# Joining the u and v tables of a PEER expert layer into one table of 8 KB rows, in a two-layer decoder step on one core

## The chip, the core and the metric

The kernel runs on one core of a Trainium2 chip. The metric is the device time of one execution in microseconds. Everything is float32. TensorE (PE in the rows) does matmuls into PSUM, VectorE (DVE) and ScalarE (ACT) the elementwise work, GpSimd (POOL) issues the gathers from HBM, SyncE (SP) issues the plain loads and stores. The core's 16 DMA engines carry all transfers.

## What is computed

Two layers over 256 prompt tokens and 8 sample tokens, width 1024. Each layer has a dense mixer (an mLSTM and a pooling group), a PEER expert layer, and a gated embedding. The expert layer is where the change sits. Each token picks 16 experts in each of 8 heads, so 128 of 16,384, and each expert has one row of 1024 floats in `u_tab` and one in `v_tab`:

```python
q = (xb @ wq).reshape(PEER_BLOCK, PEER_HEADS, 2, PEER_HALF)
s = jnp.einsum('thcd,chkd->thck', q, keys)
sv, si = lax.top_k(s, PEER_TOPK)
...
top, sel = lax.top_k(cand, PEER_TOPK)
eidx = jnp.take_along_axis(cidx, sel, axis=-1)
gate = jax.nn.softmax(top, axis=-1)
ue = u_tab[eidx]
act = jax.nn.gelu(jnp.einsum('td,thkd->thk', xb, ue))
ve = v_tab[eidx]
out = jnp.einsum('thk,thkd->td', gate * act, ve)
```

Over both layers that is 528 tokens x 128 experts x 2 rows of 4 KB, 553.7 MB out of 685 MB that the kernel moves.

## The kernel before, in words

The work is six tiles: 0 = A (tokens 0 to 127), 1 = B (tokens 128 to 255) and 2 = S (the 8 sample tokens) of layer 0, and 3, 4, 5 the same of layer 1. They run in four passes, `PASS_TILES = [[0], [1, 2], [3], [4, 5]]`. In a pass the dense front (`stage_front`: turn, norm, project, the mixer, mix, query, match, and the ranking steps rank, lists, pairs, best, soften, choose) leads to the indices of the experts. Then the experts are gathered and used, and the dense back (`stage_back`: turn3, gate, embed, apply, final) closes the layer.

Gathers. Each is one indirect DMA of 128 rows of 4 KB, one row to a partition, into a ring of `RING = 14` slots (`rows`, L1450). For a tile of 128 tokens, 128 gathers from `u` come first (gather i holds expert i of every token, so a token is a partition), then 128 from `v` (gather i holds all 128 experts of one token, so an expert is a partition). The order of all 1056 gathers is the list `GATHERS`. Gathers of u wait for the indices of their head (`best` and DVE's L2052), gathers of v for `turn_index`. Each waits also until its slot is free.

Use of a u slot. DVE multiplies it with the normed token, which ACT has put in two PSUM banks (`show`, L1633), and sums along the row (`take_dots`, L2105). The slot is then free. When all 128 products of a token are there, one gelu (L1642) and one product with the probabilities give the weights of the whole tile, PE transposes them, and DVE puts them in `wz`. Use of a v slot. PE multiplies four slots at a time (`GROUP = 4`, L1235) with 32-column windows of `wz`, two matmuls to a slot; the four slots are freed together. The sums pile up in `acc`, the same two banks that held the shown token. `add` then adds them to x, and only after it can the next tile be shown. In the last pass the last 24 tokens of tile 4 are handled in the lanes of the sample tile (`LATE`), so that the back of tile 4 can start earlier.

Order of the work. `make_schedule` weaves the list of gather steps (`groups_of`) with the dense steps, by a small table of costs (`STEPS`, `SMALL`, `ROW`, `FLIGHT`) that belongs to the kernel. Each engine then runs its part of the woven list in order. So while PE holds a dense step, the expert step behind it waits, and the other way round.

Weights. SP loads each half of a weight matrix (1 MB, 8 KB to a partition) in a ring of `WRING = 3` slots. One half, the first of the input projection, has a place of its own (`kept`) and is loaded once per layer.

## Time and profile before

| | us |
|---|---|
| three runs, median | 1912.31 |
| three runs, lowest and highest | 1903.66 and 1913.88 |
| profiled execution, first to last instruction (its span) | 1891.7 |
| DVE, POOL, PE busy in the span | 978.1, 998.2, 1079.0 |

The profile gives a span for its execution and no other time. The median of the runs stands 20.6 us above it, which covers what lies around the span and the difference between executions. The prediction sums in the span and adds those 20.6 us at the end. The rows in a later section show where the span goes. A row of a window gives start:end, length, then for PE, PE's weight loads, DVE, ACT and POOL the busy time with the number of instructions, then the granted TensorE clock (1.00 is 2.4 GHz, 0.50 is 1.2 GHz), the DMA's busy share, and GB/s. A row of a timeline gives start, length, engine and line, and in brackets the idle time before it. The trace counts each float32 matmul as two. In them, "idle before, releaser" is the time for which the engine stood still ahead of a group of instructions and who ended that; "share" of a DMA queue is the time that its packets took, as a share of 16 engines' time, and can pass 100% a little since packets overlap.

### The profile page before, as it was taken

How to read it: one execution, taken by the hardware profiler on the slowest of the kernel's cores; microseconds unless marked ns; L12 is line 12 of the kernel's file. 1: busy time of each engine (PE TensorE's matmuls, PEld its weight loads, DVE VectorE, ACT ScalarE, POOL GpSimd, SP SyncE). 2: the span in 40 equal slices, each digit the busy share in tenths (PEclk: the TensorE clock that was granted, in tenths of full speed). 3: DMA queues.
4: the chain of work that ended last, by engine and by line, in shares of the span. 5: the costliest groups of instructions: out<-in, count | busy, mean ns of one | idle time of the engine just before them, and what ended most of it. 6: DMA issues, size and time to landing. Idle time of an engine off the chain costs nothing. (4 is left out here: it accounts for less than half of the span.)

```text
span 1891.7 us, 17959 instructions
## 1 busy us (share of the span) xinstructions
PE 1079.0 (57%) x6318; PEld 499.7 (26%) x6318; DVE 978.1 (52%) x2585; ACT 192.3 (10%) x332; POOL 998.2 (53%) x1062
## 2 busy tenths in 40 slices
PE   8840257788955835385655874048885522045556
PEld 4420133433412422241112432024341211031113
DVE  1498975523445788954004576951344497850001
ACT  3200021201101200000000212000110000000002
POOL 0156534345465555656666353755446566656663
PEclk9965668789987967697676886578896765576678
DMA  8699869889999999989999799979999999999995
GB/s 333 244 359 379 337 244 410 337 359 399 357 360 406 423 410 421 404 343 419 371 366 386 256 421 365 408 286 418 368 337 366 402 374 381 396 330 372 368 367 206
DMA packets 172759, 685.11 MB, mean 362 GB/s; under 512 B 19616, under 2 KB 21344, under 8 KB 158190
## 3 DMA queue, kind: packets, MB, share of 16 engines
q0 software_dynamic: 152064, 553.72, 75.9%
q1 hardware_dynamic: 20606, 130.25, 17.3%
q8 instruction: 51, 0.84, 0.2%
q14 instruction: 38, 0.31, 0.0%
HBM read 677.66 MB, written 6.59 MB: 362 GB/s over the span
## 5 line engine op out<-in xcount | busy, mean ns | idle before, releaser
L2105 DVE SCALAR_TENSOR_TENSOR rows<-rows,acc 128x1024 f32<-128x1024 f32 x512 | 594.2, 1217 | 49.6 <-issue 26.7
L908 PE MATMUL bank<-wring,turned 128*128 128x512 f32 (+1 forms) x808 | 394.0, 635 | 40.6 <-DMA wring<-in_w 24.3
L1235 PE MATMUL acc<-rows,wz 128*32 128x512 f32 x1952 | 323.1, 783 | 143.6 <-DMA rows<-in_v,index_tb 102.6
L1450 POOL DMA_INDIRECT rows<-in_u,index_A x256 | 240.3, 939 | 303.2 <-DVE rows L2105 123.8
L1450 POOL DMA_INDIRECT rows<-in_v,index_ta x256 | 242.5, 947 | 234.1 <-PE acc L1235 142.2
L1450 POOL DMA_INDIRECT rows<-in_u,index_B x256 | 240.7, 940 | 179.1 <-DVE rows L2105 110.7
L1450 POOL DMA_INDIRECT rows<-in_v,index_tb x256 | 241.1, 942 | 138.7 <-issue 68.1
L908 PEld LDWEIGHTS bank<-wring,turned 128*128 128x128 f32 x808 | 160.5, 207 | 236.7 <-issue 205.7
L1235 PEld LDWEIGHTS acc<-rows,wz 128*32 128x32 f32 x1952 | 69.6, 130 | 351.9 <-issue 347.0
L1185 PE MATMUL bank<-xn_s,consts 128*128 128x128 f32 x256 | 48.6, 334 | 154.3 <-issue 154.3
L1185 PEld LDWEIGHTS bank<-xn_s,consts 128*128 128x128 f32 x256 | 42.9, 243 | 159.9 <-issue 159.9
L2151 DVE TENSOR_TENSOR x_b<-x_b,acc 128x1024 f32<-128x1024 f32 x2 | 2.4, 1222 | 155.8 <-issue 89.9
L905 PE MATMUL bank<-wring,turned_s 128*32 128x128 f32 x1568 | 64.9, 281 | 27.1 <-issue 27.0
L1959 DVE MAX8 top<-scratch 128x8 f32<-128x128 f32 x66 | 15.0, 282 | 120.9 <-ACT scratch L1604 119.6
L905 PEld LDWEIGHTS bank<-wring,turned_s 128*32 128x32 f32 x1568 | 44.8, 111 | 69.7 <-issue 69.6
L2141 DVE COPY wz<-w_later 128x64 f32<-128x64 f32 x4 | 0.9, 225 | 101.4 <-PE acc L1235 77.7
L1109 PE MATMUL bank<-consts,qk 128*128 128x128 f32 x64 | 12.5, 324 | 68.7 <-issue 66.3
L1194 PE MATMUL bank<-consts,dots_A 128*128 128x128 f32 x2 | 1.0, 476 | 76.6 <-issue 74.6
L2105 DVE DVE_READ_ACCUMULATOR rows<-rows,acc 128x1 f32 x512 | 42.0, 82 | 3.6 <-issue 3.6
L1136 PE MATMUL bank<-consts,top 128*128 128x128 f32 (+2 forms) x10 | 3.9, 393 | 61.9 <-DVE top_f L1993 61.9
L1259 PE MATMUL bank<-wring,emb 128*128 128x512 f32 x32 | 19.9, 781 | 26.8 <-issue 13.6
L2169 DVE TENSOR_TENSOR xn<-xn,bank 128x512 f32<-128x512 f32 x6 | 4.1, 689 | 59.9 <-PE bank L1259 59.9
(320 smaller groups left out, 1054.4 us busy)
## 6 DMA issues: line engine op xcount, KB each, us to landing
wring<-in_w SPq DMA_DIRECT2D x103, 1024.0 KB
out_sample<-scratch SPq DMA_DIRECT2D x2, 2128.5 KB
scratch<-in_c_s SPq DMA_DIRECT2D x2, 2064.0 KB
rows<-in_u,index_A POOLq DMA_INDIRECT x256
rows<-in_v,index_ta POOLq DMA_INDIRECT x256
rows<-in_u,index_B POOLq DMA_INDIRECT x256
rows<-in_v,index_tb POOLq DMA_INDIRECT x256
kept<-in_w SPq DMA_DIRECT2D x2, 1024.0 KB
```

The lines of the kernel that those rows point to most:

```text
L905: ins = pe.matmul(ps[lane_group(g), 0:P], turned["S"][:, 4 * h + c, :], w[:, c, g * P:(g + 1) * P], start=first, stop=end, skip_group_chec ...
L908: ins = pe.matmul(ps[:, part], turned["A"][:, 4 * h + c, :], w[:, c, part], start=first, stop=end, skip_group_check=True)
L1109: ins = pe.transpose(ps[:, i * P:(i + 1) * P], pq[:, 0, i * P:(i + 1) * P], const("ident"))
L1136: ins = pe.transpose(ps[0:m, i * P:(i + 1) * P], src[:, 2 * h0:2 * h1, :].rearrange("p l k -> p (l k)"), const("ident"))
L1185: ins = pe.matmul(ps[:, g * P:(g + 1) * P], const("ident")[:, lane:lane + 1].to_broadcast([P, P]), xn["S"][:, i * P:(i + 1) * P], start=Tr ...
L1235: ins = pe.matmul(acc[i * QUAD:(i + 1) * QUAD, c, :], wz[:, i, at:at + QUAD], row, start=first, stop=end, skip_group_check=True)
L1259: ins = pe.matmul(ps[:, :], emb[:, c, 0:P], w[:, 2 * j + c, :], start=(c == 0), stop=(c == 1))
L1450: pool.indirect_dma_start(out=rows[:, n % RING, :], out_offset=None, in_=a[table], in_offset=bass.IndirectOffsetOnAxis(ap=which[:, at:at + ...
L1959: highest = [marked(dve.max(values[:, 0:half], src)) for values, _, src in lists]
L2105: dve.scalar_tensor_tensor(u, u, 1.0, acc[:, :, :], ALU.mult, ALU.mult, accum_out=dots[kind][:, s:s + 1]).then_inc(u_used, 1)
L2151: after(dve.tensor_tensor(sum_, sum_, acc[:, :, :], ALU.add), acc_read)
L2169: free(dve.tensor_tensor(sig, sig, ps[:, 0:n], ALU.mult), "embed", t, j)
```

## The change

One table `uv` has the row of u and the row of v of an expert side by side, 8 KB. A gather brings 128 such rows into one of `RING = 8` slots of 8 KB a partition. There are 528 gathers in place of 1056. The ring takes 64 KB a partition in place of 56, and the 8 KB come from `kept`, which goes; the first projection half is now loaded by the weight ring in every pass.

A gather now holds 2 expert slots of 64 tokens. A tile of 128 tokens is two parts of 64 gathers; the sample tile is one part of 8 gathers of 16 experts. Inside a part the gathers go through the heads in order, 8 to a head, and the second part needs no new ranking. The indices and the probabilities are brought into that form by PE (`turn_index`, `turn_prob`, per batch of heads) and copied out by DVE.

Each gather has a chain of its own. DVE forms the products with u, ACT takes the gelu, multiplies with the probability and scales a 128x64 folding matrix to make the weights (three instructions), PE multiplies with v in two matmuls of 64 columns (four of 32 for the samples), and only then is the slot free. The token shown and the sums are in PSUM banks of their own, three in all, so `BANKS` goes from 6 to 5. At the end of a part, ACT copies the sums out, PE places them (two matmuls), and DVE adds them to x. The `LATE` handling is gone. The planner's costs for the new steps are in the same tables, and it is now told that a gather takes `ROW = 2.5` and `FLIGHT = 3.0`.

```diff
-RING = 14
-GROUP = 4
-DOTS = 2
-QUAD = 32
-TURN = QUAD // 2
+RING = 8
+STATS = 8
-LATE = (LANE - DEC) // GROUP
-BANKS = 6
+BANKS = 5
...
+TOKENS = {"A": P // 2, "B": P // 2, "S": DEC}
+PARTS = {"A": 2, "B": 2, "S": 1}
+EACH = {kind: PAIRS // (P // n) for kind, n in TOKENS.items()}
+PER_HEAD = EACH["A"] // PH
...
+    return [(t, part, i) for p in range(4) for t in PASS_TILES[p] for part in range(PARTS[KIND[t]]) for i in range(EACH[KIND[t]])]
...
+    for g in GATHERS:
+        if g[0] not in PASS_TILES[p]:
+            continue
+        if g[2] == 0:
+            out.append(("show", *g[:2]))
+        out.append(("dots", *g))
+        if behind:
+            summed()
+        behind = g
+    summed()
...
-ROW, HALF_LOAD, ISSUE, FLIGHT, SIGNAL = 1.28, 2.5, 1.0, 2.0, 0.1
+ROW, HALF_LOAD, ISSUE, FLIGHT, SIGNAL = 2.5, 2.5, 1.0, 3.0, 0.1
...
-        rows = sb("rows", P, RING, D)
-        kept = sb("kept", P, 4, BLOCK)
+        rows = sb("rows", P, RING, 2 * D)
...
-        acc = ctx.enter_context(nc.psum_tensor("acc", [P, 2, BLOCK], F32))
+        shown = ctx.enter_context(nc.psum_tensor("shown", [P, 2, BLOCK], F32))
+        acc = ctx.enter_context(nc.psum_tensor("acc", [P, BLOCK], F32))
...
+            def vals(t, part, i):
+
+                kind, n = KIND[t], PLACE[t, part, i]
+                first, end = i == 0, i + 1 == EACH[kind]
+                nth = PARTS_IN_ORDER.index((t, part))
+                if first and nth:
+                    pe.wait_ge(acc_read, nth)
+                pe.wait_ge(weights_ready, n + 1)
+                row = rows[:, n % RING, D:2 * D]
...
+                    for c in range(2):
+                        ins = pe.matmul(acc[c * 64:(c + 1) * 64, :], weighted[:, n % STATS, :], row[:, c * BLOCK:(c + 1) * BLOCK],
+                                        start=first, stop=end, skip_group_check=True)
+                ins.then_inc(v_used, 1)
...
-            for n, (table, t, i) in enumerate(GATHERS):
+            for n, (t, part, i) in enumerate(GATHERS):
                 kind = KIND[t]
...
+                if kind != "S" and part == 0 and i % PER_HEAD == 0:
+
+                    emptied(pool, "turn_index", t, batch_of("turn_index", t, i // PER_HEAD)[2])
                 if n >= RING:
 
-                    old = GATHERS[n - RING]
...
+                    pool.wait_ge(v_used, n - RING + 1)
                 pool.indirect_dma_start(
-                    out=rows[:, n % RING, :], out_offset=None, in_=a[table],
-                    in_offset=bass.IndirectOffsetOnAxis(ap=which[:, at:at + 1], axis=0),
+                    out=rows[:, n % RING, :], out_offset=None, in_=a["uv"],
+                    in_offset=bass.IndirectOffsetOnAxis(ap=index[kind][:, part, i:i + 1], axis=0),
                 ).then_inc(row_in[n % RING], 16)
...
+            def dots_weights(t, part, i):
+
+                kind, n = KIND[t], PLACE[t, part, i]
+                of_row = dots[kind][:, part, i:i + 1]
+                act.wait_ge(u_used, n + 1)
+                after(act.activation(of_row, of_row, ACT.Gelu_apprx_tanh))
...
+                after(act.activation(of_row, of_row, ACT.Copy, scale=share[kind][:, part, i:i + 1]))
+                if n >= STATS:
+                    act.wait_ge(v_used, n - STATS + 1)
...
+                    ins = act.activation(weighted[:, n % STATS, :], const("fold"), ACT.Copy, scale=of_row)
+                ins.then_inc(weights_ready, 1)
...
+            def take_dots(t, part, i):
+
+                kind, n = KIND[t], PLACE[t, part, i]
+                if i == 0:
+                    dve.wait_ge(xn_shown, PARTS_IN_ORDER.index((t, part)) + 1)
+                dve.wait_ge(row_in[n % RING], 16 * (n // RING + 1))
+                u = rows[:, n % RING, 0:D].rearrange("p (c n) -> p c n", c=2)
+                dve.scalar_tensor_tensor(u, u, 1.0, shown[:, :, :], ALU.mult, ALU.mult,
+                                         accum_out=dots[kind][:, part, i:i + 1]).then_inc(u_used, 1)
...
-        "u": f["peer_u"].reshape(DEPTH * EXPERTS, D),
-        "v": f["peer_v"].reshape(DEPTH * EXPERTS, D),
+        "uv": np.concatenate([f["peer_u"], f["peer_v"]], axis=2).reshape(DEPTH * EXPERTS, 2 * D),
```

Three places show how the instructions move. The first is PE from the end of tile 3's experts into tile 4. Before, `acc<-rows,wz` are the products with v, `x_a` is the turning of tile 3 for its gates (turn3), `wring,turned` its gates, `wring,emb` the embedding, and `bank<-xn_s,consts` copies of the sample tokens.

```order
L1235 MATMUL acc<-rows,wz 32x512 x32
L884 MATMUL bank<-consts,x_a 128x128 x8
L908 MATMUL bank<-wring,turned 128x512 x16
L1259 MATMUL bank<-wring,emb 128x512 x8
L1255 MATMUL bank<-wring,emb 32x128 x16
L1185 MATMUL bank<-xn_s,consts 128x128 x64
L1194 MATMUL bank<-consts,dots_B 128x128
L1235 MATMUL acc<-rows,wz 32x512 x208
```

In the changed kernel `acc<-rows,weighted` are the products with v (two to a gather), `summed` the placing of a part's sums, and `shown` the showing of tokens.

```order
L1202 MATMUL acc<-rows,weighted 64x512 x70
L1212 MATMUL bank<-summed,consts 64x512 x2
L1177 MATMUL shown<-xn_b,consts 64x512 x4
L865 MATMUL bank<-consts,x_a 128x128 x8
L889 MATMUL bank<-wring,turned 128x512 x16
L1239 MATMUL bank<-wring,emb 128x512 x4
L1202 MATMUL acc<-rows,weighted 64x512 x4
L1239 MATMUL bank<-wring,emb 128x512 x4
L1235 MATMUL bank<-wring,emb 32x128 x16
L1202 MATMUL acc<-rows,weighted 64x512 x122
```

Before, the gates and the embedding stood ahead of u gathers that PE does not touch. Now they stand ahead of the first product of the next tile, which every slot waits for.

The second is ACT in the ranking of tile 0 and the front of pass 1. `best` is the softmax's exponential, `gate_exp_f_s` and `gate_ln_f_s` belong to the forget gates. The rows of the changed kernel:

```order
L1575 ACT_TABLE_LOAD
L1575 ACTIVATE best<-best 128x32
L1582 ACT_TABLE_LOAD
L1582 ACTIVATE dots_A<-dots_A 128x1
L1587 ACTIVATE dots_A<-dots_A,share_A 128x1
L1593 ACTIVATE weighted<-consts,dots_A 128x64
L1582 ACTIVATE dots_A<-dots_A 128x1
L1587 ACTIVATE dots_A<-dots_A,share_A 128x1
L1593 ACTIVATE weighted<-consts,dots_A 128x64
```

Before, ACT had one row for the gelu of a tile (`L1642 ACTIVATE dots_A<-dots_A 128x128`). Now there are three instructions for every gather, and a table load each time the gelu follows another function: 102 table loads in all in place of 51.

The third is PE at the end of the last pass. Before, `rows,wz 32x256` are the 24 late tokens and `rows,wz_s` the samples:

```order
L1235 MATMUL acc<-rows,wz 32x512 x208
L884 MATMUL bank<-consts,x_b 128x128 x8
L1226 MATMUL acc<-rows,wz 32x256 x16
L908 MATMUL bank<-wring,turned 128x512 x8
L1226 MATMUL acc<-rows,wz 32x256 x16
L908 MATMUL bank<-wring,turned 128x512 x4
L1226 MATMUL acc<-rows,wz 32x256 x16
L908 MATMUL bank<-scratch,turned 128x512 x4
L1226 MATMUL acc<-rows,wz 32x256 x48
L1226 MATMUL acc<-rows,wz_s 32x256 x32
```

And in the changed kernel, where `rows,weighted 32x256` are the samples, four to a gather:

```order
L1202 MATMUL acc<-rows,weighted 64x512 x2
L1212 MATMUL bank<-summed,consts 64x512 x2
L865 MATMUL bank<-consts,x_b 128x128 x8
L1198 MATMUL acc<-rows,weighted 32x256 x4
L889 MATMUL bank<-wring,turned 128x512 x12
L889 MATMUL bank<-scratch,turned 128x512 x4
L1198 MATMUL acc<-rows,weighted 32x256 x28
L865 MATMUL bank<-consts,x_s 128x128 x2
```

Before, 32 gathers of 4 KB rows ran beside the back of tile 4. Now 8 gathers of 8 KB rows do.

## Rows read from the trace of the kernel before

**Rows 1.** The page's busy time by engine.

```profile
PE 1079.0 (57%) x6318; PEld 499.7 (26%) x6318; DVE 978.1 (52%) x2585; ACT 192.3 (10%) x332; POOL 998.2 (53%) x1062
```

**Rows 2.** Busy time by window: start, the four passes, the end.

```profile
0.00:86.00 86.00, 76.18 (x251) 41.55 (x252) 25.56 (x98) 22.69 (x36) 2.37 (x6) 1.00 0.77 284
86.00:561.00 475.00, 281.97 (x1884) 138.11 (x1886) 294.78 (x914) 60.15 (x111) 242.32 (x257) 0.77 0.91 353
561.00:997.00 436.00, 250.17 (x1068) 107.90 (x1064) 231.75 (x578) 36.53 (x57) 256.36 (x273) 0.75 0.99 395
997.00:1459.00 462.00, 287.06 (x2035) 135.41 (x2026) 250.94 (x679) 51.19 (x93) 240.45 (x256) 0.76 0.94 361
1459.00:1869.00 410.00, 172.09 (x897) 69.45 (x897) 172.63 (x309) 17.38 (x26) 255.81 (x273) 0.66 0.97 370
1869.00:1891.00 22.00, 11.54 (x196) 7.22 (x196) 2.39 (x8) 4.37 (x9) 0.90 (x1) 0.81 0.27 105
```

**Rows 3.** DMA queues over the whole span: packets, MB, share.

```profile
q0 software_dynamic: 152064, 553.72, 75.9%
q1 hardware_dynamic: 20606, 130.25, 17.3%
```

**Rows 4.** DMA queues, window 600 to 700.

```profile
q0 software_dynamic: 7516, 27.37, 66.9%
q1 hardware_dynamic: 2199, 14.74, 35.0%
```

**Rows 5.** DMA queues, window 1730 to 1739, gathers alone.

```profile
q0 software_dynamic: 1033, 3.76, 102.3%
```

**Rows 6.** Windows with gathers alone: v, v, u.

```profile
905.00:1005.00 100.00, 56.29 (x310) 12.97 (x311) 1.22 (x1) 0.00 (x0) 65.65 (x71) 0.70 0.97 368
1690.00:1830.00 140.00, 75.93 (x416) 15.94 (x416) 0.76 (x4) 0.00 (x0) 92.70 (x100) 0.72 0.97 366
1200.00:1250.00 50.00, 0.47 (x1) 0.18 (x1) 38.65 (x69) 1.59 (x2) 32.79 (x35) 0.50 1.00 391
```

**Rows 7.** Timeline of POOL.

```profile
86.11 1.08 POOL L1450 DMA_INDIRECT rows<-in_u,index_A  x1 [83.20 <-DVE index_A L2052]
...
1060.86 0.93 POOL L1450 DMA_INDIRECT rows<-in_u,index_A  x1 [24.88 <-DVE rows L2105]
...
1711.30 0.94 POOL L1450 DMA_INDIRECT rows<-in_v,index_tb  x1 [0.30 <-issue]
...
1715.45 0.94 POOL L1450 DMA_INDIRECT rows<-in_v,index_tb  x1 [3.22 <-remote]
```

**Rows 8.** Timeline of PE: two groups of v and one gate step.

```profile
1710.05 3.48 PE L1235 MATMUL acc<-rows,wz 128*32 128x512 f32 x16 [3.07 <-DMA rows<-in_v,index_tb]
...
1715.04 1.93 PE L1235 MATMUL acc<-rows,wz 128*32 128x512 f32 x16 [1.51 <-DMA rows<-in_v,index_tb]
...
1849.34 3.70 PE L908 MATMUL bank<-wring,turned 128*128 128x512 f32 x8
```

**Rows 9.** Groups by line in pass 0, window 86 to 561.

```profile
L2105 DVE SCALAR_TENSOR_TENSOR rows<-rows,acc 128x1024 f32<-128x1024 f32 x128 | 148.1, 1217 | 5.5 <-issue 2.3 <-remote 1.9 <-DVE mixer L1819 0.6
...
L1450 POOL DMA_INDIRECT rows<-in_u,index_A x128 | 120.0, 938 | 193.8 <-DVE index_A L2052 113.6 <-DVE rows L2105 48.4 <-issue 28.9
...
L1235 PE MATMUL acc<-rows,wz 128*32 128x512 f32 x485 | 72.7, 691 | 6.1 <-issue 2.7 <-DMA rows<-in_v,index_ta 2.0 <-DVE w_later L2136 0.7
```

**Rows 10.** Timeline of the end: ACT, POOL, PE, DVE.

```profile
1862.00 1.28 ACT L1470 ACT_TABLE_LOAD   x1
...
1863.30 0.29 ACT L1470 ACTIVATE r_root<-r_in,consts 128x1 f32<-128x1 f32 x1
...
1868.96 0.93 POOL L1450 DMA_INDIRECT rows<-in_v,index_S  x1 [0.31 <-issue]
...
1876.75 3.39 PE L1226 MATMUL acc<-rows,wz_s 128*32 128x256 f32 x32 [3.71 <-DMA rows<-in_v,index_S]
...
1889.03 0.48 DVE L1734 SCALAR_TENSOR_TENSOR x_s<-x_s,inv_s,gain 128x256 f32<-128x256 f32 x1
```

518 lines of the change are left out of this document (204 added, 314 removed).

## The prediction

> **What bounds the kernel now.** I read the busy times first: no engine is busy for even 60% of the span [rows 1]. Then the span cut at the first gather of each pass [rows 2]: from pass 0 on, the DMA's share is 0.91 to 0.99. Then what a full DMA moves. With gathers alone and no stall, the gather queue has a share of 102.3% and moves 3.76 MB in 9 us, 418 GB/s [rows 5]; beside weights the two queues together move 42.1 MB in 100 us, 421 GB/s [rows 4]. I take 420 as full. The four passes run at 353, 395, 361 and 370 GB/s [rows 2], so they lose, against a full DMA, 475 x (1 - 353/420) = 76 us, 26, 65 and 49 us. The 86 us ahead of the first gather move 284 GB/s and lose 28; the end, from the last issue on, some 17. That is 261 us over the time of a full DMA, and the kernel's time is the DMA's plus these losses. So the change is to be judged by the DMA time of its bytes and by each loss.
>
> What the losses are. In pass 0 POOL waited 193.8 us ahead of its u gathers, 113.6 for indices [rows 9]. Of these, 83.2 are the start [rows 7], the other 30 are two gaps where the ranking was late: DVE had 148 us of products with u in this pass [rows 9] beside the ranking, 295 us busy in all [rows 2]. In pass 2 one gap of 24.88 us is put down to DVE's products [rows 7]: the next tile can't be shown before the last v of the sample tile is added, since both use the same two banks. In passes 1 and 3 the stretches of v alone run at 366 to 368 GB/s with a DMA share of 0.97 [rows 6]. There POOL issues every 1.24 us (0.94 and 0.30 of idle), which is the pace of the DMA (0.524 MB in 1.25 us), and stands still for 3.22 us now and then [rows 7]. Such a loss is never made good, for neither can run ahead.
>
> **The change, part by part.**
>
> Gathers of 8 KB rows. The bytes stay. The trace has no gather of such rows; the nearest are the weight loads, mostly 8 KB rows, which move 14.74 MB for a share of 35.0%, 421 GB/s at full share, where gathers of 4 KB rows beside them move 27.37 MB for 66.9%, 409 [rows 4]. Gathers take 75.9% of 1891.7 us, 1436 us [rows 3]. By the ratio 0.971 they take 41 us less; the other bound is no gain. I take 41, since the row length is all that the two differ in there. The Trainium skill (DMA: Bandwidth & Descriptors, Why small descriptors are slow) has a fixed overhead of about 3 cycles to a packet of 32-byte beats. By it 4 KB cost 131 cycles and 8 KB 259, and the gain would be 1.1%, 16 us in place of 41.
>
> POOL. 528 issues in place of 1056. At 1.24 us each [rows 7] against about 2.43 us of DMA time for 1.05 MB it is no longer level with the DMA. A stall of 3.22 us then leaves it room to catch up.
>
> `kept` goes. Two halves of 1 MB are loaded again, and the constants grow by 0.1 MB: 5 us.
>
> The start. The first gather now also waits for PE to turn the indices and DVE to copy them: some 2 us for small matmuls and a copy.
>
> DVE. A product with u is still 1.22 us and 0.08 for the sum's readout, for the same bytes; but it now comes once in 1.05 MB in place of once in 0.52. Over pass 0 its sum stays, over the ranking it halves: beside the first 36 or so gathers of 1 MB stand 36 products in place of 72, so the ranking has 44 us more of DVE, and a pair of heads covers 16 gathers, 39 us. I count the two index gaps, 27 us of the 30, as gone, and 9 more of the waits on DVE: pass 0 loses 40 in place of 76.
>
> Shown tokens and sums in banks of their own. The gap in pass 2 goes, 22 of its 25 us. Its place is taken by the gates of the tile before: with the embedding they stand on PE ahead of the first product with v of the next tile. That is 4 gate steps of 3.70 us at full clock [rows 8], the embedding and the turning, about 25 us, and some 5 more where samples go with it. Eight slots of DMA time are 19 us, so each of three tile changes starves the gathers by about 10 us, of which the weight halves fill a part. I count 8 us for each. With a steadier flow elsewhere, pass 1 stays at 26, pass 2 goes from 65 to 36, and pass 3, where 3.22 us stalls go and 8 us come, from 49 to 25.
>
> The chain of a slot. From the last issue to PE's start on its rows are 7.8 us [rows 10]; with 1.25 us more to transfer, 9. Then DVE 1.3, ACT three small instructions of 0.29 [rows 10], about 1, and PE. A switch of ACT's table takes 1.28 us [rows 10]; there are 51 more of them, 65 us over the span on an engine that is busy for 192 [rows 1], and each lies in one slot's chain. PE: a group of four slots in 32 columns takes 1.93 us at full clock, 3.48 at the lower [rows 8], so 0.48 to a slot. A step of 8 wide matmuls takes 3.70 [rows 8], so four such would be 1.85. In 64 columns the price lies between 0.48 and 1.85; I take the middle of the doublings, 0.95. The Trainium skill (TensorEngine Tiling (Array Packing), Theoretical Speedup) has up to 4 times for 32 columns and up to 2 times for 64: by it also the price doubles, and it speaks against the change. All told a slot is away for 12 to 14 us, against 8 x 2.43 = 19.4: a cover of 5 to 7 us. If a step of DVE or PE ahead of a product is longer than that, its excess comes on top.
>
> PE as a whole. In pass 0 it is busy for 282 us, 73 of these with v [rows 2, 9]. With 128 x 0.95 in place of 73 it is 330 in a pass of 429, 77%, where it is at 59% now. This is the tightest place of the forecast.
>
> The end. Now 8 gathers, 19 us, run beside the back of tile 4, where 32 gathers of 0.5 MB, 40 us, did. The gates of tile 4 (14.8 us), its update and norm (7) end about 13 us after the last row landed; the last three sample gathers come behind them on DVE and ACT (5), and from the end of the samples' last product (1880.1) it is 11.6 us to the end of the span, the last norm at 1889.03 within it [rows 10], as now. That makes 29 in place of 15: 14 us more.
>
> Sum: -41 + 5 + 2 - 36 + 0 - 29 - 24 + 14 = -109. From the span of 1891.7 that is 1783, and with the 20.6 us between the span and the median of the runs 1803.
>
> **The rivals.**
>
> (a) The forecast; its losses may be 30 to 50 us off to either side: 1755 to 1840. Chance 0.48.
>
> (b) Rows go as two packets of 4 KB. Today's 152,064 packets of that queue [rows 3] are one to each of the 135,168 rows and 16 small ones to each of the 1056 gathers, and nothing shows a longer one there. Against it: the other queue has 8 KB rows, and no more packets than such rows need. Then the 41 us stay: 1844. Chance 0.07. The Trainium skill (DMA: Bandwidth & Descriptors, SWDGE vs HWDGE vs iDMA) says that packets of GpSimd's queue are preferably at most 4096 B; no row here shows more.
>
> (c) Gathers alone keep today's pace. What ends the 3.22 us stall is put down to "remote", so I don't know that it scales with the issues. In the new order some 236 gathers run with nothing beside them. At the pace of u alone, 391 GB/s [rows 6], each takes 2.68 us, 0.25 more than at full DMA, together 59; 20 of these are in my losses, so 1842. At that of v, 367, it is 101, so 1884. Chance 0.19.
>
> (d) Slower: the chain over three engines holds both streams back. PE runs its list in order, and each product with v now waits for a gather that has just landed, while the dense steps behind it wait too. PE's busy time in passes 0 to 2, with the 73 us of v replaced by 0.95 a gather in each, would be 330, 306 and 336 us. At the share it had in pass 2, 287 of 462 [rows 2], these take 532, 494 and 542 us; with the start, a pass 3 of 376, the end and the 20.6 us the total is near 2080. It decides against the change when PE's share in these passes stays under 0.70, for then the three take over 1395 us and the total passes 1912; the forecast, with 429, 425 and 425 us, needs 0.76. For it: order and prices are planned with a flight of 3 us. Against it: with weights and gathers together the DMA was full for 100 us [rows 4], so the weave does work. Chance 0.20, most of it slower.
>
> (e) Gains and losses cancel, 1900 to 1920: 0.06.
>
> **How the numbers follow.** Half a per cent, 10 us, is about what a measurement of this kernel tells from no change. Faster: (a), (b), (c) and a little of (d), 0.76. Same: 0.07. Slower: 0.17. The predicted time is that of (a), 1803, its own range 1755 to 1840. The range for 8 in 10 leaves out (d) above 1895 and a little below (a): 1755 to 1895.
>
> **What would show it.** The gather queue: half the packets, a share near 74% of 1891.7 us of time (1395 us) for the same MB; if its packets are as many as now, (b). Gathers alone (late in passes 1 and 3) near 425 GB/s; under 395 it is (c). POOL's waits for indices after the start near zero. At each tile change a dip in the DMA behind the gates. PE's share in passes 0 to 2 near 0.76, and products with v at 0.5 to 1.9 us a gather at full clock. The prediction is wrong if DMA slices in the mixed stretches fall to 8 tenths and below while PE waits on ACT and ACT on DVE.

## The result, and the profile after

The changed kernel takes 1792.75 us, the median of 4 runs (1789.11 to 1795.90), beside 1910.24 us (1903.66 to 1913.88, 4 runs) for the kernel before on the same chip. The ratio is 0.936, 95% interval 0.931 to 0.941: faster, inside the range, 10 us under the 1803 that I gave. The profiled execution has a span of 1790.6 us and a time of 1792.79.

The page of the changed kernel, to be read beside [rows 1, 3]: busy times, then the two DMA queues with packets, MB and share.

```profile
PE 1364.3 (76%) x6310; PEld 501.9 (28%) x6310; DVE 992.0 (55%) x2540; ACT 692.9 (39%) x1965; POOL 498.0 (28%) x532
...
q0 software_dynamic: 76032, 553.68, 74.8%
q1 hardware_dynamic: 20606, 132.36, 18.3%
```

POOL is busy for half of what it was. The gather queue moves the same MB in half the packets (76,032 are 528 x 128 rows and 528 x 16 small ones), for a share of 74.8% of 1790.6 us, 1339 us, where it was 1436 and I expected 1395. PE's share goes from 57% to 76%, ACT's from 10% to 39%.

Windows of the changed kernel, cut near the first gather of each pass (94.81, 539.99, 952.90 and 1378.64) and at the last issue, as in [rows 2].

```profile
0.00:97.00 97.00, 80.42 (x264) 43.31 (x264) 25.83 (x100) 24.88 (x39) 2.09 (x6) 0.98 0.72 270
97.00:540.00 443.00, 339.48 (x1986) 147.73 (x1988) 293.75 (x906) 188.34 (x504) 119.61 (x128) 0.85 0.92 376
540.00:953.00 413.00, 315.09 (x1032) 101.94 (x1028) 229.19 (x550) 157.60 (x463) 127.97 (x137) 0.84 0.99 415
953.00:1379.00 426.00, 344.66 (x2076) 142.78 (x2078) 255.19 (x677) 178.04 (x496) 121.21 (x129) 0.86 0.96 393
1379.00:1744.00 365.00, 255.91 (x716) 51.65 (x712) 171.70 (x280) 124.78 (x422) 126.91 (x136) 0.70 0.98 411
1744.00:1791.00 47.00, 28.71 (x240) 14.48 (x240) 16.31 (x31) 19.23 (x43) 0.27 (x1) 0.83 0.31 128
```

The passes run at 376, 415, 393 and 411 GB/s, where they ran at 353, 395, 361 and 370. A full DMA now moves 427 GB/s. This is seen where gathers are alone, in pass 3; the stretches of v alone made 366 to 368 before [rows 6]. The window, and the gather queue in it:

```profile
1690.00:1740.00 50.00, 34.05 (x84) 5.19 (x80) 25.57 (x42) 16.92 (x61) 18.88 (x21) 0.69 1.01 427
...
q0 software_dynamic: 2925, 21.34, 101.0%
```

Against 427 the losses are: start 97 x (1 - 270/427) = 36 us, the passes 53, 12, 34 and 14, the end 33, together 181. The 687.26 MB take 1610 us of a full DMA, and 1610 + 181 is the span of 1790.6.

One gather's chain in that stretch, on DVE, ACT and PE, and a later product of PE (timeline; in brackets the idle time ahead and what ended it).

```profile
1704.36 1.22 DVE L2068 SCALAR_TENSOR_TENSOR rows<-rows,shown 128x1024 f32<-128x1024 f32 x1 [1.22 <-DMA rows<-in_uv,index_B]
...
1705.62 0.20 ACT L1582 ACTIVATE dots_B<-dots_B 128x1 f32<-128x1 f32 x1 [1.54 <-DVE rows L2068]
...
1706.18 0.35 ACT L1593 ACTIVATE weighted<-consts,dots_B 128x64 f32<-128x64 f32 x1
...
1706.58 1.97 PE L1202 MATMUL acc<-rows,weighted 128*64 128x512 f32 x4 [0.47 <-ACT weighted L1593]
...
1711.50 1.08 PE L1202 MATMUL acc<-rows,weighted 128*64 128x512 f32 x4 [0.64 <-ACT weighted L1593]
```

The chain runs once in about 2.46 us, 1.05 MB at 427 GB/s. Each of its engines waits for the one ahead, so none of them sets the pace here. The two matmuls (four in the trace) take 1.08 us at full clock, at 1711.50, and 1.97 at the lower.

POOL's waits over the whole span (total, times, longest):

```profile
POOL rows L1399 <- PE acc L1202: 1086.9, 388, 29.2
POOL rows L1399 <- DVE index_A L2047: 99.5, 2, 94.4
```

Of the 1086.9 us that POOL waits for slots most costs nothing, since the DMA is full meanwhile: the four passes lose 112 us together. Waits for indices are 99.5 us in two times, 94.4 of them the start, so about 5 are left of the 30 behind it. The products with v and the table loads on the page (busy us, mean ns, idle before):

```profile
L1202 PE MATMUL acc<-rows,weighted 128*64 128x512 f32 x2048 | 699.5, 789 | 268.6 <-ACT weighted L1593 257.2
...
L1582 ACT ACT_TABLE_LOAD x41 | 52.6, 1283 | 49.1 <-DVE rows L2068 48.8
```

### The profile page after: what moved, and what is told of

It reads as the page before. It is cut to its first block and busy times, and to the rows that moved or that the text cites. A ratio compares the mean times of both kernels' runs of the same rounds, so it can differ in the third digit from the quotient of the medians.

```text
span 1790.6 us, 19308 instructions
## 1 busy us (share of the span) xinstructions
PE 1364.3 (76%) x6310; PEld 501.9 (28%) x6310; DVE 992.0 (55%) x2540; ACT 692.9 (39%) x1965; POOL 498.0 (28%) x532
## 2 busy tenths in 40 slices
DMA packets 96737, 687.26 MB, mean 384 GB/s; under 512 B 11104, under 2 KB 12640, under 8 KB 14318
## 3 DMA queue, kind: packets, MB, share of 16 engines
q0 software_dynamic: 76032, 553.68, 74.8%
## 5 line engine op out<-in xcount | busy, mean ns | idle before, releaser
L1202 PE MATMUL acc<-rows,weighted 128*64 128x512 f32 x2048 | 699.5, 789 | 268.6 <-ACT weighted L1593 257.2
L2068 DVE SCALAR_TENSOR_TENSOR rows<-rows,shown 128x1024 f32<-128x1024 f32 x528 | 632.7, 1220 | 381.5 <-DMA rows<-in_uv,index_B 249.5
L1399 POOL DMA_INDIRECT rows<-in_uv,index_A x256 | 242.4, 947 | 722.6 <-PE acc L1202 585.7
L1399 POOL DMA_INDIRECT rows<-in_uv,index_B x256 | 240.4, 939 | 496.6 <-PE acc L1202 474.4
L1202 PEld LDWEIGHTS acc<-rows,weighted 128*64 128x64 f32 x2048 | 134.6, 162 | 731.1 <-ACT weighted L1593 619.7
L1582 ACT ACTIVATE dots_B<-dots_B 128x1 f32<-128x1 f32 x256 | 51.6, 202 | 359.8 <-DVE rows L2068 354.6
L1593 ACT ACTIVATE weighted<-consts,dots_A 128x64 f32<-128x64 f32 x256 | 89.0, 348 | 8.4
L1593 ACT ACTIVATE weighted<-consts,dots_B 128x64 f32<-128x64 f32 x256 | 89.0, 348 | 8.4
L1587 ACT ACTIVATE dots_A<-dots_A,share_A 128x1 f32<-128x1 f32 x256 | 75.3, 294 | 8.3
L1587 ACT ACTIVATE dots_B<-dots_B,share_B 128x1 f32<-128x1 f32 x256 | 75.3, 294 | 8.3
```

What stands on the lines that cost most here:

```text
L1202: ins = pe.matmul(acc[c * 64:(c + 1) * 64, :], weighted[:, n % STATS, :], row[:, c * BLOCK:(c + 1) * BLOCK], start=first, stop=end, skip_g ...
L1399: pool.indirect_dma_start(out=rows[:, n % RING, :], out_offset=None, in_=a["uv"], in_offset=bass.IndirectOffsetOnAxis(ap=index[kind][:, pa ...
L1582: after(act.activation(of_row, of_row, ACT.Gelu_apprx_tanh))
L1587: after(act.activation(of_row, of_row, ACT.Copy, scale=share[kind][:, part, i:i + 1]))
L1593: ins = act.activation(weighted[:, n % STATS, :], const("fold"), ACT.Copy, scale=of_row)
L2068: dve.scalar_tensor_tensor(u, u, 1.0, shown[:, :, :], ALU.mult, ALU.mult, accum_out=dots[kind][:, part, i:i + 1]).then_inc(u_used, 1)
```

## The experiments

They ran in three rounds. In the first (two_issues, two_halves, early_free, half_v) the kernel before took 1891.27 us (1876.00 to 1902.25, 7 runs), and the changed kernel itself wasn't run. The second and third ran on one other chip (before: 1908.22 and 1911.88); the changed kernel ran again in the second, and is the base of both. So for the runs of the first round a difference to the base crosses chips, and the kernel before differs by 0.9% between the two chips. Ratios are to the kernel before of the same round. I tell the runs in the order of the questions.

**The base.**

> The changed kernel itself, unaltered, on the chip of this call, since the kernel before took 1891 us here and 1910 on the first chip. Every theory: its ratio to before is 0.93 to 0.95; the time 1785 to 1797 us. It is the base for the other three of this call.

1786.95 us (1783.52 to 1792.68), ratio 0.936 (0.9286 to 0.9435). It came out as expected, and the differences below are to 1786.95 us. In its own traced execution the span is 1781.7 us.

### Why the gathers got faster: row length or number of issues

**Two gathers of 4 KB to a slot.**

```diff
-                pool.indirect_dma_start(
-                    out=rows[:, n % RING, :], out_offset=None, in_=a["uv"],
-                    in_offset=bass.IndirectOffsetOnAxis(ap=index[kind][:, part, i:i + 1], axis=0),
-                ).then_inc(row_in[n % RING], 16)
+                for table, lo in (("u", 0), ("v", D)):
+                    pool.indirect_dma_start(
+                        out=rows[:, n % RING, lo:lo + D], out_offset=None, in_=a[table],
+                        in_offset=bass.IndirectOffsetOnAxis(ap=index[kind][:, part, i:i + 1], axis=0),
+                    ).then_inc(row_in[n % RING], 16)
...
```

> The changed kernel, but each slot is filled by two gathers of 4 KB rows, from the separate tables u and v, in place of one gather of 8 KB rows. Bytes, slots, order and chains stay; 1056 issues and twice the packets come back. Theory A (row length and number of issues made the faster stretches of gathers alone): beside weights the DMA falls from 427 to about 420 GB/s, 11 us; the gathers alone, about 236 of 528, 247 MB, go at 366 to 391 GB/s in place of 427, 54 to 97 us. Together 1855 to 1895 us. Theory B (the new order of the work made them faster, whatever the rows are): only the packets' rate counts, 687 MB at 418 in place of 427 GB/s, 35 us at most: 1800 to 1828 us.

2029.63 us (2017.70 to 2034.72), ratio 1.073 (1.063 to 1.083). Both theories missed it: the new order without the joined rows is slower than the kernel before. By slices a part of the loss lies in the mixed stretches, with 257 to 323 GB/s in many; which wait makes them so low I didn't separate. The page's 40 slices and gather queue:

```profile
GB/s 319 252 303 271 318 348 358 295 402 353 357 257 323 422 382 421 400 324 389 360 360 270 307 421 383 380 353 306 315 339 372 252 383 384 359 369 369 367 369 68
...
q0 software_dynamic: 152064, 553.72, 71.4%
```

The seven slices ahead of the last, gathers alone, are at 359 to 384, as v alone before [rows 6], and the best slice is 422. POOL stops as in [rows 7]:

```profile
1890.14 0.94 POOL L1400 DMA_INDIRECT rows<-in_u,index_B  x1 [3.69 <-issue]
```

**Two gathers of 64 rows to a slot.**

```diff
+                for lo in (0, 64):
...
+                        out=rows[lo:lo + 64, n % RING, :], out_offset=None, in_=a["uv"],
+                        in_offset=bass.IndirectOffsetOnAxis(ap=index[kind][0:64, part, i:i + 1], axis=0),
```

> The changed kernel, but each slot is filled by two gathers of 64 rows of 8 KB (the upper 64 partitions get the rows that the indices of the lower 64 name, so other experts are used there). 1056 issues again, but packets of 8 KB. If the number of issues made the slow stretches (POOL level with the DMA at 1.24 us an issue), gathers alone fall under 400 GB/s and the time is 1850 to 1890 us as with two issues of 4 KB rows; it is less if an issue of 64 rows is shorter. If the row length did it, the time stays at 1790 to 1800 us.

2741.02 us (2611.51 to 2823.88; the trace is of the run of 2611.51). It tells nothing on the question, for it brought something else. The gather queue in a stretch of 45 us of gathers alone, late in pass 3:

```profile
q0 software_dynamic: 1528, 10.01, 101.4%
```

At full share the queue moves 10.01 MB in 45 us, 222 GB/s in place of 427: gathers of 64 rows into one half of the partitions go at half the rate. In the packet records an 8 KB packet takes 600 ns there (median) and 309 ns in the changed kernel. Both halves of a slot read the same rows in this run; whether that has a part in it, no run tells. The Trainium skill (DMA: Bandwidth & Descriptors, Rules for kernel authors) says of transfers to two partition halves that they serialize and share the same engines, so one transfer of 128 partitions should be used. The advice holds here; that the two halves together cost about twice the one is more than the page says.

**A tiny gather behind each.**

```diff
+                if n >= 4 * RING:
+                    pool.wait_ge(extra_in, 16 * (n - 4 * RING + 1))
+                pool.indirect_dma_start(
+                    out=extra[0:16, n % (4 * RING), :], out_offset=None, in_=a["uv"].rearrange("r (k c) -> (r k) c", c=4),
+                    in_offset=bass.IndirectOffsetOnAxis(ap=index[kind][0:16, part, i:i + 1], axis=0),
+                ).then_inc(extra_in, 16)
...
```

> The changed kernel with a second, tiny indirect gather (16 rows of 16 bytes, into a place that nobody reads) behind each gather of 8 KB rows: 1056 issues as before the change, with the bytes and the packet length of the changed kernel. It tells the number of issues from the row length in the run with two gathers of 4 KB rows to a slot (2030 us, gathers alone at 367 to 369 GB/s with stops of POOL of 3.1 to 3.7 us). If the number of issues, POOL being level with the DMA, makes the stops and the slow stretches behind them: gathers alone fall to 370 to 400 GB/s and the time rises to 1850 to 1950 us. If the length of the rows does it: gathers alone stay over 415 GB/s and the time is at most 20 us over the base.

2025.98 us (2022.51 to 2032.00), ratio 1.060 (1.052 to 1.069): 239 us over the base, with rows of 8 KB. The direction is that of the first theory, the time 76 us beyond its range. The ratio is 1.060 where two gathers of 4 KB gave 1.073, and the intervals overlap, so the length of the rows is worth about 1% here, if anything. So it is the issues. A window of gathers alone, then POOL's timeline at one stop:

```profile
1850.00:1950.00 100.00, 65.02 (x144) 9.94 (x144) 43.03 (x70) 30.35 (x108) 61.82 (x70) 0.59 0.94 370
```

```profile
1898.75 0.95 POOL L1401 DMA_INDIRECT rows<-in_uv,index_B  x1 [0.30 <-issue]
...
1901.16 0.95 POOL L1401 DMA_INDIRECT rows<-in_uv,index_B  x1 [0.30 <-issue]
1902.42 0.85 POOL L1407 DMA_INDIRECT extra<-in_uv,index_B  x1 [0.30 <-issue]
1907.00 0.95 POOL L1401 DMA_INDIRECT rows<-in_uv,index_B  x1 [3.73 <-PE acc L1204]
```

An issue of 8 KB rows and a tiny one take 2.41 us together (1898.75 to 1901.16), the DMA 2.46 for the rows. Then POOL stands for 3.73 us, put down to PE. The packets of single gathers show that this isn't a slot (worked out from the trace's packet records, in us; packets are dealt to the gathers in the order of their starts; first and last packet are counted from the end of the issue, with the shortest start set to 1.3 us):

```
kernel, gathers alone       issue ends   first packet starts   last packet ends
changed, gather 512            1707.33         +10.49              +13.19
changed, gather 514            1712.08         +10.65              +13.35
extra issues, gather 496       1885.24          +3.77               +6.59
extra issues, gather 502       1899.70          +4.17               +6.92
before, gather 998             1782.04          +4.02               +5.40
```

The gather issued behind the stop, at 1907.00, needs the slot of the eighth before it, gather 496. That landed at 1891.8, and PE's product with it was over at 1896.7, more than 6 us before POOL's stop began. In the changed kernel a queue of 10 us of transfers stands ahead of the DMA; in the two others it is 4, and a stop of 3 to 4 us empties it. The same stop stands in the kernel before every 16 issues in its stretches of v alone (898 to 989 and 1743 to 1835). Two of them, 16 issues apart, and the 40 slices of 1745 to 1775 (0.75 us each):

```profile
1743.36 0.94 POOL L1450 DMA_INDIRECT rows<-in_v,index_tb  x1 [3.39 <-PE acc L1235]
...
1766.20 0.93 POOL L1450 DMA_INDIRECT rows<-in_v,index_tb  x1 [3.29 <-PE acc L1235]
...
GB/s 218 339 279 289 333 295 300 279 279 344 404 399 404 399 415 426 415 426 410 426 421 421 421 415 421 421 426 415 415 360 131 218 388 240 333 289 284 328 300 350
```

16 gathers of 0.524 MB in 22.84 us are 367 GB/s. That is the 366 to 368 of [rows 6] whole: in those stretches POOL with its stops was the bound, and the DMA, which falls to 131 GB/s after a stop, only looked full on average. Here too the slot was free: at the second of these stops POOL stood from 1762.9 on, and PE had been done with the slot at 1759.7. The pace of 1.24 us alone isn't the loss. Where u was gathered alone, POOL made 40 issues without such a stop (1176.70 to 1225.12), and the DMA kept up 420 GB/s:

```profile
1200.00:1226.00 26.00, 0.00 (x0) 0.00 (x0) 25.58 (x46) 0.00 (x0) 19.61 (x21) 0.50 1.03 420
```

So the 391 of [rows 6] is no pace of u: its window takes in the first gathers of v, from 1227 on. What makes POOL stop, and why not there, is open. The trace calls it "remote", "issue" or the last engine that signalled.

**A tiny gather behind every second.**

```diff
+                if n % 2:
+                    continue
...
```

> The changed kernel with the tiny extra gather behind every second gather only: 792 issues. POOL then needs 1.24 us and 1.15 more for every second, 1.8 us to a gather of 1.05 MB, against 2.46 us of DMA time; with an extra behind each it needed 2.4, level with the DMA, and the kernel took 239 us more. If what counts is that POOL is level with the DMA (it can't build a queue that covers its stops, nor refill the ring behind a long wait), the cost is far under half: 10 to 60 us over the base of 1787, gathers alone at 420 or more. If each issue costs its share wherever it stands, it is half of 239: 1890 to 1920.

1825.71 us (1823.87 to 1831.35), ratio 0.956 (0.950 to 0.963): 39 us over the base for 264 issues more, where the next 264 cost 200. Gathers alone:

```profile
1600.00:1700.00 100.00, 69.08 (x176) 11.99 (x172) 51.09 (x84) 34.62 (x123) 54.71 (x61) 0.70 1.01 426
```

They run at 426 GB/s, and both this and the time are as the first theory expected. So the tiny transfers themselves take nothing of the rate here, and the issues cost little as long as POOL has time to spare, and much once it is level with the DMA. Where the 39 us lie I didn't separate; slower refilling of the ring behind the longer waits fits them, and was only argued.

### What the chain of a slot costs

**Six slots.** `RING = 6` in place of 8.

> The changed kernel with a ring of 6 slots in place of 8; the sums and all steps stay. A slot is away for 12 to 14 us by my count, and 6 slots are 14.7 us of DMA time, so a steady stretch of gathers alone should still run at 420 or more, with no cover left; each of the longer waits in the mixed stretches then costs 4.9 us more. There are about 30 of over 7 us ahead of POOL. My theory: gathers alone over 415 GB/s, 80 to 150 us more in all, 1870 to 1940. Rival (a slot is away for longer than I count): gathers alone fall under 400 GB/s. Rival (the ring isn't what the losses hang on, as freeing slots at DVE's product gained 1 per cent only): under 40 us more.

1867.55 us (1865.41 to 1870.33), ratio 0.978 (0.970 to 0.985): 81 us over the base, at the lower edge of my theory (80 us more; its 1870 is missed by 2). Gathers alone:

```profile
1740.00:1800.00 60.00, 41.73 (x98) 6.60 (x100) 29.80 (x49) 20.68 (x74) 22.73 (x25) 0.64 1.01 428
```

They keep 428 GB/s with 6 slots. So a slot is away for no more than 6 x 2.46 = 14.8 us besides waiting in the queue, and the two further slots are cover for the mixed stretches, as I took them.

**The slot free at DVE's product.**

```diff
-                row = rows[:, n % RING, D:2 * D]
+                row = consts[:, AT["ones"][0]:AT["ones"][0] + D]
...
-                    pool.wait_ge(v_used, n - RING + 1)
+                    pool.wait_ge(u_used, n - RING + 1)
```

> The changed kernel, but PE multiplies the weights with constants in place of the rows' v half, and a slot is free when DVE's product with u is done. So the chain over ACT and PE no longer holds a slot, and engines have the same work. Theory A (with 8 slots the chain is covered but for the steps that stand ahead of the products with v, some 8 us at a tile change and several of 5 to 10 us in passes 0 and 2): the passes lose 112 us now against a full DMA of 427 GB/s, and I expect 50 to 70 of these back, 1725 to 1745 us. Rival (the losses come where DVE or the indices hold the gathers, not PE and ACT): under 20 us, 1775 or more.

1776.29 us (1773.31 to 1779.62), ratio 0.939 (0.931 to 0.947). In time it is 11 us under the base of the other chip and 16 under the first result; by the ratio (the base has 0.936) it is no faster. So the gain lies between nothing and 16 us. My theory (50 to 70) fell; the rival held. The reason stands on DVE, at the change from tile 0 to tile 1:

```profile
571.01 0.69 DVE L2098 TENSOR_TENSOR xn_a<-xn_a,bank 128x512 f32<-128x512 f32 x1 [19.35 <-PE bank L1239]
```

DVE itself stands still for 19.35 us for the embedding, with the next tile's products behind it in its list, and POOL's longest wait grows to 32.5 us, as its waits show:

```profile
POOL rows L1399 <- DVE rows L2068: 1062.3, 373, 32.5
```

That ACT and PE hold the slot adds little to it, 16 us at most.

**Half of the products with v.**

```diff
-                    for c in range(2):
+                    for c in range(1 if 0 < i < EACH[kind] - 1 else 2):
```

> The changed kernel, with one of the two products with v left out for all but the first and last gather of a part, so half of the sums are wrong; PE has some 300 us less of work and the slot's chain is 0.5 to 1 us shorter. If PE as a whole is near the bound (share 0.77 to 0.81 in passes 0 to 2), 40 to 80 us are gained, 1715 to 1750 us. If PE only costs by single long waits ahead of a product, as I hold, 5 to 25 us: 1768 to 1788.

1787.41 us (1785.74 to 1792.85), ratio 0.945 (0.937 to 0.953). In time it is the base. But it didn't take PE's time away. Its page has

```profile
L1202 PE MATMUL acc<-rows,weighted 128*64 128x512 f32 x1056 | 702.6, 790 | 262.7 <-ACT weighted L1593 254.3
```

so 1056 matmuls are busy for 702.6 us where 2048 were for 699.5, and PE as a whole for 1368.6. Ends of matmuls are modelled, so here is an event that waits for the real end: POOL's next issue, which needs the slot of the product. A product at full clock in the changed kernel is the row at 1711.50 above (1.08 us, two matmuls), and POOL's issue behind it:

```profile
1712.86 0.94 POOL L1399 DMA_INDIRECT rows<-in_uv,index_B  x1 [0.78 <-PE acc L1202]
```

The same in this run, with one matmul:

```profile
1712.03 1.07 PE L1202 MATMUL acc<-rows,weighted 128*64 128x512 f32 x2 [0.54 <-ACT weighted L1593]
...
1713.38 0.94 POOL L1399 DMA_INDIRECT rows<-in_uv,index_B  x1 [0.67 <-PE acc L1202]
```

From PE's start to POOL's are 1.36 us with two matmuls and 1.35 with one. The two halves of 64 columns lie side by side in time, and one alone takes as long as both. So the run says nothing on a lighter PE.

**No gelu in the chain.** `ACT.Copy` in place of `ACT.Gelu_apprx_tanh`.

> The changed kernel with a copy in place of the gelu in every gather's chain, so the weights are products without it. The instruction stays, the switch of ACT's table goes: 41 table loads of 1.28 us (52.6 us in all) fewer, some at the head of a slot's chain. Since a slot freed at DVE's product gained only about 11 us, I expect 2 to 12 us less than the base, 1775 to 1785. Rival (ACT's chain sets the mixed stretches, as in my fourth rival): 30 us or more less.

1777.00 us (1773.46 to 1779.00), ratio 0.930 (0.924 to 0.936): 10 us under the base, as expected. But 56 table loads went, not the 41 ahead of a gelu alone: 46 are left of 102, since a function that follows no gelu often needs no load either (the exponential has 6 for 10). ACT is busy for 623.8 us in place of the base's 692.7. These 69 us less of ACT gave 10, so its chain doesn't set the mixed stretches.

### Order of the lists

**Products between the gate steps.**

```diff
+def between_gates(order):
...
+        if e[0] == "gate":
+            for _ in range(16 if e[1:] == (3, 1, 1, 4) else 2):
+                k = next((k for k, f in enumerate(rest) if f[0] in ("dots", "vals", "show", "place")), None)
+                if k is not None and rest[k][0] in ("dots", "vals"):
+                    out.append(rest.pop(k))
...
```

> The changed kernel with another order at the tile changes alone: behind each gate step stand the next two entries of the next tile's gathers (a product with u, or weights and products with v), and all that is left of the last sample tile goes ahead of tile 4's update and last norm. In the changed kernel DVE waited 15 to 20 us for the embedding there with these products behind it, and POOL 24.9, 29.2 and 25.8 us; at the end the three last sample products began at 1771.3, some 20 us after their rows had landed. Theory (the stop is one of order, on DVE and ACT as much as on PE): POOL's three stops shorten to under 15 us, some 5 us less each, and the end is 8 to 12 us shorter; 15 to 27 us under the base. Rival (the weight halves fill the gaps, and the table loads that the mixing adds on ACT, 1.28 us each, eat the rest): within 8 us of the base.

1775.10 us (1773.19 to 1777.21), ratio 0.929 (0.922 to 0.936): 12 us under the base, between theory and rival. The expectation had both the tile changes and the end in it. POOL and DVE of the changed kernel at the first tile change, and then this one's POOL there and its PE at the end:

```profile
574.53 1.10 POOL L1399 DMA_INDIRECT rows<-in_uv,index_B  x1 [24.91 <-PE acc L1202]
...
571.12 0.69 DVE L2098 TENSOR_TENSOR xn_a<-xn_a,bank 128x512 f32<-128x512 f32 x1 [17.25 <-PE bank L1239]
```

```profile
560.25 0.94 POOL L1416 DMA_INDIRECT rows<-in_uv,index_B  x1 [11.70 <-PE acc L1219]
...
1735.78 0.64 PE L1215 MATMUL acc<-rows,weighted 128*32 128x256 f32 x8
1736.35 3.70 PE L906 MATMUL bank<-wring,turned 128*128 128x512 f32 x8
```

POOL's waits of 24.9 and 29.2 us became 11.7 and 10.6; the third was split in two before (25.8 and 17.0) and is 13.4 and 20.5 now. A part only moved: behind the second change POOL now waits 19.8 us at 1016.25, where it waited 8.6. From the last issue (1730.53) to the end are 44.6 us, where the base has 46.0 (1735.74 to 1781.7) in its profile. So at most 2 of the 12 us come from the end, and about 9 from what lies between: from the end of pass 0 (the issues at 536.70 and 533.03) to the last issue are 1193.8 us, where the base has 1202.7.

**The exponentials at their price.** `"soften": (("DVE", 0.4), ("ACT", 3.5))` in the planner's table.

> The changed kernel with one number of the planner changed: ACT's cost for the exponentials of the probabilities, 0.5 us before, 3.5 now (the trace has two table loads of 1.28 us around it, and DVE waited 17.3 us in 7 times for it in pass 0, with products behind it; one of these is at 171 to 176 us, where the DMA then moved nothing for some 6 us). If those waits of DVE and PE on ACT are a part of the 53 us that pass 0 loses: 4 to 15 us faster than the base. If other work stands in their place: within 4 us of it.

1785.84 us (1784.89 to 1788.57): 1 us under the base, no effect. The waits it was to remove are still there (pass 0), 15.2 us where the base has 15.3:

```profile
DVE shares L2034 <- ACT best L1575: 15.2, 6, 5.6
```

ACT's timeline in the changed kernel shows what I had misread:

```profile
171.24 1.28 ACT L1444 ACT_TABLE_LOAD   x1 [3.38 <-DVE gate_abs_f L1709]
...
172.75 1.28 ACT L1445 ACT_TABLE_LOAD   x1
...
174.27 1.28 ACT L1575 ACT_TABLE_LOAD   x1
```

Three table loads stand in a row, and two are for the exponential and the logarithm of the mixer's gates, which stand ahead in ACT's list. The planner's price of the third moves nothing there.

**Both, and a shorter end.**

```diff
+for _e in (("place", 5, 0), ("turn3", 5)):
+    SCHEDULE.remove(_e)
+    SCHEDULE.insert(SCHEDULE.index(("final", 4)), _e)
```

> The order of the run gates (12 us under its base), with the samples' last sums placed and turned ahead of tile 4's last norm (their sum waited from about 1757 to 1760.7 there), and the planner's 3.5 us for the exponentials. As a sum of its parts: 12 for the gates, 2 to 4 for the end, 0 to 15 for the exponentials: 1756 to 1775 us, ratio 0.920 to 0.929. It tells whether the order of the lists still holds losses.

1772.72 us (1771.72 to 1780.45), ratio 0.929 (0.922 to 0.936). Nothing of the computation is left out in it, and by its median it is the fastest of these, inside the range expected, though the exponentials gave nothing. Its last norm ends 38.7 us after its last issue (1728.70 to 1767.42 in its timeline), where it was 42.4 with the gates alone (1730.53 to 1772.93). Of these 4 us the medians have 2.4, and the ranges overlap.

## Why the prediction was right, and where its steps were not

The sum gave a span of 1783 us, the trace has 1790.6. Of my 188 us of losses 181 were found; the full DMA's 1595 us were 1610. The mechanisms that I counted on are there, but the closeness is partly luck. By part the losses are 36, 53, 12, 34, 14 and 33 us (start, four passes, end) where I had 30, 40, 26, 36, 25 and 31: 13 too few in pass 0 and 14 too many in pass 1 cancel, and the 20.6 us at the end were added for a wrong reason, as told below.

**Gathers of 8 KB rows: mis-sized.** I took 0.971 from 409 beside 421 GB/s in [rows 4], 41 us. Gathers alone make 427 where 4 KB rows without a stop make 418 [rows 5] to 422 (the best slice with two gathers to a slot), and 420 over 26 us of u. That is 1.2 to 2.1% of 1316 us at 421, so 16 to 28 us. At these rates the whole transfer is 1610 us in place of 1631 (at 420), with 2 MB more. The wrong step was to divide by the share. Packets overlap, and those of 4 KB more: alone they show 102.3% at 418 GB/s [rows 5], which is 409 at full share, my figure again, with nothing beside them; those of 8 KB show 101.0% at 427. The Trainium skill (DMA: Bandwidth & Descriptors, Why small descriptors are slow) has about 3 cycles to a packet, by which I had estimated 1.1% and 16 us; that is at the lower edge of the 16 to 28, nearer than my row.

**POOL: the right mechanism, and about half of the change.** I wrote that POOL is no longer level with the DMA and has room to catch up, and that 3.22 us stalls go. I priced it at part of 24 us in pass 3 and nothing in pass 1. The passes 1 and 3 lost 26 and 49 us and lose 12 and 14, together 49 of the 101 us of span. That is 14 us in pass 1 that I didn't count and 11 more in pass 3. With the issues put back, the same kernel takes 239 us more; 370 in place of 427 GB/s for the 236 gathers alone would be some 90 of them, and the rest lies in the mixed stretches, where I didn't separate it. I had taken the stops for something that comes "now and then"; I hadn't seen that they stand every 16 issues and are all that the v stretches lack to 420, because the DMA's share there was 0.97.

**`kept` and the start.** The reload is within the 1610 us. The start loses 36 us where I had 30 and the first gather stands at 94.81, 8.7 later than [rows 7], where I gave 2. PE turned the indices (from 93.80 on) behind a projection of 7.03 us, so that DVE waited 3.33 us for them, and the ranking itself ended later:

```profile
86.84 7.03 PE L889 MATMUL bank<-wring,turned 128*128 128x512 f32 x16
...
94.35 0.17 DVE L2047 CAST index_A<-bank 128x16 uint32<-128x16 f32 x1 [3.33 <-PE bank L1144]
```

In its own trace the base began 4 us earlier (90.2 us of wait), so a part of it differs between executions.

**Pass 0: half right.** The index gaps went, as said (99.5 - 94.4 = 5 us left). But it loses 53 us in place of 40. And what I had written as the sign of being wrong did come in one stretch of it, 130 to 225: the DMA's share falls to 0.74 and 0.71, and 33 of the 53 us are lost there.

```profile
130.00:180.00 50.00, 35.49 (x148) 18.08 (x144) 21.78 (x48) 20.38 (x47) 9.72 (x11) 0.84 0.74 298
180.00:225.00 45.00, 28.41 (x146) 8.67 (x148) 35.19 (x131) 21.17 (x59) 11.62 (x13) 0.61 0.71 254
...
176.56 0.61 PE L1144 MATMUL bank<-prob,consts 128*64 128x16 f32 x8 [5.95 <-DVE prob L2042]
```

In it PE waits 12.0 us for ACT's weights and ACT 22.5 us for DVE's products, while DVE, with the ranking and the products, is busy for 35 of the last 45 us. The last row is a gap where PE waited for the probabilities, with products that had their rows behind it. This is rival (d)'s mechanism, in one stretch. No run took it away, so what the chain costs there against the ranking itself is open.

**Tile changes.** Each was to starve the gathers for about 10 us, of which I counted 8. The DMA's slices at the first (530 to 590, 1.5 us each) dip twice, by about 5 and 2 us:

```profile
GB/s 404 426 421 120 0 0 158 399 404 426 421 426 426 421 431 421 426 421 426 431 426 426 421 431 437 415 262 306 289 218 421 431 412 443 427 405 423 430 426 426
...
531.98 1.02 PE L1161 MATMUL bank<-consts,by_head 64*128 64x8 f32 x4 [6.69 <-DVE by_head L2040]
```

Only the second dip, of 2 us, stands behind the gates. The first comes ahead of them, behind the ranking of the samples, for which PE waited 6.69 us at 531.98. At the second change (982 to 998) the dips sum to some 6 us, at the third (1410 to 1442) to some 14; there the DMA moves next to nothing from 1433 to 1440, and PE stands for 11.33 us ahead of the embedding, a wait that I hadn't foreseen. So 24 us in three were about 22, but not 8 each. The engine was right only in part: I named PE's gates, but DVE waited 17.25 us for the embedding with its products behind that. Pass 2 loses 34 (36 forecast).

**The slot's chain.** Six slots still carried 428 GB/s, so a slot is away for at most 14.8 us; my 12 to 14 fit that and aren't shown more closely. The product with v takes 1.08 us at full clock, where I took 0.95 between 0.48 and 1.85. The switches of ACT's table are 51 more, as said (102 and 51); with 56 of them gone, 10 us go.

**The end.** I gave 29 us behind the last row's landing. By its packets the last row landed at about 1759, so it is 32. What filled them was in part something else: the samples' last three products stood on DVE behind B's update and last norm, 15 to 19 us after their rows by the packets (1752.4, 1754.9 and 1758.6), and their gates and norm came after. The runs gates and best took a few of these back.

```profile
1769.96 1.28 DVE L1696 SCALAR_TENSOR_TENSOR x_b<-x_b,inv,gain 128x1024 f32<-128x1024 f32 x1
1771.29 1.22 DVE L2068 SCALAR_TENSOR_TENSOR rows<-rows,shown 128x1024 f32<-128x1024 f32 x1
...
1777.67 0.42 DVE L2074 TENSOR_TENSOR x_s<-x_s,acc 128x256 f32<-128x256 f32 x1 [2.88 <-PE acc L1198]
```

**The 20.6 us.** This step failed. The profiled execution of the changed kernel took 2.2 us more than its span. So the 20.6 us weren't around the span: with 2.2 us more, before's profiled execution took 1894, under all its four runs of that round, and most of the 20.6 was scatter. That kernel scatters by up to 1.4% within a round, the changed one by 0.5%. 1783 + 2 would have been 8 us under the result, 1803 was 10 over.

**The rivals.** (b) fell with the packets' number: 76,032 are 144 to a gather, so a row of 8 KB is one packet. (c) fell: gathers alone make 427. It had named the right unknown, the 3.22 us stop. (d) fell as the decider, though it holds in the stretch of pass 0 above: PE's share in passes 0 to 2 is 0.77, 0.76 and 0.81, where the forecast needed 0.76 and the break-even was 0.70. (e) fell.

## What to carry to other kernels

Compare the engine that issues transfers with the transfers themselves. With 1.24 us to an issue and 1.25 to its transfer, a stop of 3.3 us every 16 issues cost 12 to 14% of the rate while the DMA showed 97% busy; with half the issues the queue in front of the DMA covers every stop. A slot's chain over three engines waits where any of the three lists has a long step ahead of it; freeing the slot earlier wins little while DVE stands in front of the next product. And the share of a queue is no price for its bytes, since its packets overlap.

## What was new of the hardware

- POOL's gathers stop for 3 to 4 us with their slot free: every 16 issues in the stretches of v alone of the kernel before, and every 24 to 28 in places with the tiny ones between. 40 issues of u in a row had no such stop (1176.70 to 1225.12). With 528 issues of 8 KB rows gathers alone showed no trace of it in their rate.
- Gathers of 64 rows of 8 KB into one half of the partitions each, both halves reading the same rows, run at 222 GB/s, gathers of 128 rows at 427.
- Two matmuls of 64 columns in different column halves take the time of one. That is the 2 times of the Trainium skill (TensorEngine Tiling (Array Packing), Theoretical Speedup), now shown by leaving one out: POOL is released 1.36 us after PE's start with both and 1.35 with one.
- Gathers alone move 427 GB/s with rows of 8 KB, 418 to 422 with rows of 4 KB where POOL doesn't stop.
